# First attention of a six-stage block: softplus, triangular sums and exp, or sigmoids, a reversed scan and transposed blocks

## The reference, cut to what matters

```python
def stick_breaking_attention(q, k, v):
    """A[t,s] = beta_ts * prod_{s<j<t}(1 - beta_tj), s < t."""
    for i in range(seq // Q_BLOCK):
        q0 = i * Q_BLOCK
        kv_len = q0 + Q_BLOCK
        z = jnp.einsum('bqhd,bkhd->bhqk', q[:, q0:kv_len], k[:, :kv_len]).astype(jnp.float32) * scale
        causal = k_pos < q_pos
        log_beta = jax.nn.log_sigmoid(z)
        log_1m = jnp.where(causal, log_beta - z, 0.0)
        later = lax.cumsum(log_1m, axis=3, reverse=True) - log_1m
        w = jnp.where(causal, jnp.exp(log_beta + later), 0.0)
        outs.append(jnp.einsum('bhqk,bkhd->bqhd', w.astype(v.dtype), v[:, :kv_len]))
```

## Time and profile before

| | |
|---|---|
| median of 3 runs | 1973.13 us (1972.97 to 1973.66) |
| the profiled execution | 1974.07 us, its span 1972.3 us |
| granted TensorE clock, mean | 0.997 |
| busy: TensorE, weight loads, VectorE, ScalarE, GpSimd | 1940.5, 1582.1, 1470.6, 953.6, 454.8 us |
| the first attention's loop over pairs | about 734 to 846 us of the span |

### The profile page before, as it was taken

The page is one execution under the profiler, slowest core; times in us unless marked ns, Lnnn a source line. Parts: engine busy times, 40 slices in busy tenths (PEclk is TensorE's granted clock), DMA queues, the critical chain, the costliest instruction groups (busy, mean ns, idle before and its releaser), DMA issues.

```text
span 1972.3 us, 27125 instructions
## 1 busy us (share of the span) xinstructions
PE 1940.5 (98%) x10176; PEld 1582.1 (80%) x10176; DVE 1470.6 (75%) x2123; ACT 953.6 (48%) x1541; POOL 454.8 (23%) x471
## 2 busy tenths in 40 slices
PE   9999999999999999999999999999999999999997
PEld 6777878898897776787889889788888888886666
DVE  8995477877785449757786778778778778437985
ACT  5574343333344348733333335565555555236774
POOL 4131100570171000010066036124333331000002
PEclk9999999999999999999999999999999999999998
DMA  8465322243233220022324224322222223322112
GB/s 291 112 140 161 106 77 97 64 145 92 75 108 117 87 95 11 1 88 86 99 75 145 86 70 115 91 71 59 86 85 77 81 65 107 98 79 72 36 38 75
DMA packets 84546, 180.57 MB, mean 92 GB/s; under 512 B 18240, under 2 KB 33984, under 8 KB 84416
## 3 DMA queue, kind: packets, MB, share of 16 engines
q1 hardware_dynamic: 80848, 172.08, 29.1%
q0 software_dynamic: 3424, 6.23, 1.2%
q10 hardware_dynamic: 144, 0.52, 0.1%
HBM read 171.53 MB, written 7.27 MB: 91 GB/s over the span
## 4 chain that ended last, share of the span: by engine, by line
PE 68%; DVE 18%; ACT 6%; issue 6%; DMA 1%; SPq 0%; DVEq 0%; ACTq 0%
PE psum L522 12%; PE psum L525 12%; PE psum L523 12%; DVE wl L418 3%; ACT wh L406 3%; PE psum L462 3%; PE psum L459 3%; PE psum L460 3%; PE psum L563 2%; PE psum L566 2%; PE psum L564 2%; PE psum L544 2%; PE psum L1090 1%; PE psum L1092 1%; PE psum L1091 1%
## 5 line engine op out<-in xcount | busy, mean ns | idle before, releaser
L418 DVE TENSOR_TENSOR wl<-raw,wh 128x1024 fp32r<-128x1024 f32 (+3 forms) x359 | 430.8, 1203 | 255.1 <-ACT wh L406 254.2
L522 PE MATMUL psum<-xh,wh 128*128 128x512 f32 x1376 | 543.2, 395 | 1.8 <-DVE xl L641 1.8
L525 PE MATMUL psum<-xh,wl 128*128 128x512 f32 x1376 | 537.0, 390 | 2.5 <-DVE wl L418 2.5
L523 PE MATMUL psum<-xl,wh 128*128 128x512 f32 x1376 | 535.7, 389 | 0.0
L406 ACT ACTIVATE wh<-raw 128x1024 fp32r<-128x1024 f32 (+3 forms) x359 | 345.0, 964 | 291.1 <-PE psum L525 98.9
L522 PEld LDWEIGHTS psum<-xh,wh 128*128 128x128 f32 x1376 | 258.4, 188 | 61.2 <-ACT wh L406 2.6
L525 PEld LDWEIGHTS psum<-xh,wl 128*128 128x128 f32 x1376 | 258.3, 188 | 60.2 <-DVE wl L418 6.3
L523 PEld LDWEIGHTS psum<-xl,wh 128*128 128x128 f32 x1376 | 258.4, 188 | 55.2 <-issue 2.4
L431 POOL TENSOR_TENSOR raw<-raw 128x256 f32<-128x256 f32 x78 | 74.0, 949 | 441.1 <-DMA raw<-d_w 441.1
L462 PE MATMUL psum<-fh,wl 128*128 128x256 f32 x546 | 154.9, 284 | 1.8 <-DVE wl L418 1.6
L459 PE MATMUL psum<-fh,wh 128*128 128x256 f32 x546 | 154.7, 283 | 1.2 <-DVE fl L965 1.0
(11 more groups left out here) (548 smaller groups left out, 3710.3 us busy)
## 6 DMA issues: line engine op xcount, KB each, us to landing
raw<-d_w SPq DMA_DIRECT2D x224, 512.0 KB, 3.6
raw<-d_w SPq DMA_DIRECT2D x126, 256.0 KB, 2.7
Mt<-d_kd SPq DMA_DIRECT2D x64, 64.0 KB, 2.5
raw<-d_w SPq DMA_DIRECT2D x8, 320.0 KB, 2.9
bc<-d_bc SPq DMA_DIRECT2D x8, 256.0 KB, 4.5
d_ud<-ust SPq DMA_DIRECT2D x8, 256.0 KB, 2.6
U<-d_ud POOLq DMA_DIRECT2D x64, 32.0 KB, 2.4
d_yd<-HY SPq DMA_DIRECT2D x64, 32.0 KB, 2.1
```

Of the source, the lines that this page charges most:

```text
L418: dve.e.tensor_tensor(K.wl[n % NH][:, 0:w], K.raw[n % RAW][:, o:o + w], K.wh[n % NH][:, 0:w].bitcast(F32), ALU.subtract).then_inc(K.S["lo" ...
L522: pe.e.matmul(b[:, :], WH[:, o:o + P], XH, start=(k == k0), stop=False)
L523: pe.e.matmul(b[:, :], WH[:, o:o + P], XL, start=False, stop=False)
L525: mm = pe.e.matmul(b[:, :], WL[:, o:o + P], XH, start=False, stop=(k == k1 - 1))
```

## The change

Query and key change places: a block n = 4p + i now is pair p and query block i, with the query on the partition and 128(i+1) keys on the columns, for both heads. So there are 32 blocks. For each: scores and mask (`scores_pe`), ScalarE's two sigmoids (`sigmoid_act`: beta to SBUF, 1 - beta in place in PSUM), a scan of products from the last key back on VectorE (`remain_dve`), GpSimd's multiply of beta by what is left (`weigh_pool`), transposes of the 128x128 blocks of both heads on TensorE into two fixed banks (`turn1_pe`), and a copy of them to `ww` (`turned_act`). `mix_pe` works per pair as before. The sums, their constants `tri`, the softplus and the high and low parts are gone. There are three beta buffers, two for what is left, two pairs of score banks and one pair of turn banks.

```diff
-def sums_pe(K, pe, p, part): ...
-def softplus_act(K, act, i): ...
-def weigh_act(K, act, i): ...
-def softplus_abs_dve(K, dve, p): ...
-def softplus_dve(K, dve, i): ...
+TURN_BANK, SPREAD_BANK = 4, 6
+def score_bank(n):
+    return 2 - n % 2 * 2
+def keys(n):
+    return P * (n % 4 + 1)
+def scores_pe(K, pe, n):
+    p, i = n // 4, n % 4
+    pe.wait_ge("kq", 8 + p + 1)
     for e in range(2):
+        take(pe, score_bank(n) + e, ("rem", n + 1))
+    for e in range(2):
+        r = slice(64 * e, 64 * e + 64)
+        pe.e.matmul(scores(K, n)[:, e, :], K.qT[r, p, i * P:(i + 1) * P], K.kT[r, p, 0:keys(n)], start=True, stop=False,
+                    skip_group_check=True)
+    for e in range(2):
+        mm = pe.e.matmul(scores(K, n)[:, e, i * P:(i + 1) * P], K.mkb[:, :], K.idb[:, :], start=False, stop=True,
                          skip_group_check=True)
     mm.then_inc(K.S["sc"], 1)
+def sigmoid_act(K, act, n):
+    z = scores(K, n)
+    act.wait_ge("sc", n + 1)
+    act.wait_ge("trn", n - 2)
+    act.other("sigmoid")
+    act.e.activation(beta(K, n), z, ACT.Sigmoid).then_inc(K.S["act"], act.up())
+    act.e.activation(z, z, ACT.Sigmoid, scale=-1.0).then_inc(K.S["sgm"], 1)
+def remain_dve(K, dve, n):
+    z, out = scores(K, n), K.left[n % 2]
+    dve.wait_ge("sgm", n + 1)
+    dve.wait_ge("wgt", n - 1)
+    for e in range(2):
+        mm = dve.e.tensor_tensor_scan(out[:, e, 0:keys(n)][:, ::-1], z[:, e, :][:, ::-1],
+                                      K.zero[:, 0:1].broadcast_to([P, keys(n)]), 1.0, ALU.mult, ALU.add)
+    mm.then_inc(K.S["rem"], 1)
+def weigh_pool(K, pool, n):
+    k = keys(n)
+    w = beta(K, n)[:, :, 0:k - 1]
+    pool.wait_ge("rem", n + 1)
+    pool.e.tensor_tensor(w, w, K.left[n % 2][:, :, 1:k], ALU.mult).then_inc(K.S["wgt"], 1)
+def turn1_pe(K, pe, n):
     for e in range(2):
+        take(pe, TURN_BANK + e, ("wg", n + 1))
+    pe.wait_ge("wgt", n + 1)
+    for e in range(2):
+        for j in range(n % 4 + 1):
+            c = slice(j * P, (j + 1) * P)
+            mm = pe.e.transpose(K.bank[TURN_BANK + e][:, c], beta(K, n)[:, e, c], K.con("ident"))
+    mm.then_inc(K.S["trn"], 1)
+def turned_act(K, act, n):
+    p, i = n // 4, n % 4
+    act.wait_ge("trn", n + 1)
+    act.wait_ge("mix", p - 1)
+    act.e.activation(K.ww[:, p % 2, :, i:4 * i + 1:3, :],
+                     K.psum[:, TURN_BANK:TURN_BANK + 2, 0:keys(n)].rearrange("p e (j c) -> p e j c", c=P),
+                     ACT.Copy).then_inc(K.S["wg"], 1)
...
-LATE_HEADS = {2: ((0, 0), (1, 1)), 3: ((2, 5), (3, 6))}
+LATE_HEADS = {7: 0, 9: 1, 11: 2, 13: 3}
 def att1_pe(K, pe):
...
+    for t in range(2, 32):
+        scores_pe(K, pe, t)
+        if t == 2:
             head_sums_pe(K, pe, 3, 7)
+        if t in LATE_HEADS:
+            head_spread_pe(K, pe, 3, LATE_HEADS[t], SPREAD_BANK)
+        if t >= 3:
+            turn1_pe(K, pe, t - 3)
+        if t % 4 == 0 and t >= 8:
+            mix_pe(K, pe, t // 4 - 2)
+    turn1_pe(K, pe, 29)
     x = x_of(K, pe, 5)
     last = product_steps(K, pe, "b_w_o", (0, 1), (2, 3), x, (("h", 17), ("h", 18)))
+    next(last)
+    turn1_pe(K, pe, 30)
+    mix_pe(K, pe, 6)
+    next(last)
+    next(last)
+    turn1_pe(K, pe, 31)
+    next(last)
+    next(last)
     mix_pe(K, pe, 7)
 def att1_act(K, act):
...
+    for t in range(2, 35):
+        if t < 32:
+            sigmoid_act(K, act, t)
+        if t == 4:
             head_rsqrt_act(K, act, 3)
+        if t >= 3:
+            turned_act(K, act, t - 3)
+        if t % 4 == 1 and t >= 9:
+            mixed_act(K, act, t // 4 - 2)
```

More of the change, by code:

```diff
@@ L345 @@
     + ["gcp", "conv", "fa", "gv", "fh", "fl"]
-    + ["hcp", "hsq", "hn", "hny", "hbc", "kq", "mk", "sc", "sp2", "spa", "spl", "sums", "wg", "mix", "vt"]
+    + ["hcp", "hsq", "hn", "hny", "hbc", "kq", "mk", "sc", "sgm", "rem", "wgt", "trn", "wg", "mix", "vt"]
     + ["mraw", "dtk", "mxs", "mset", "mseta", "msetp", "mci", "mcv", "mth", "mfin", "mz", "mzt", "mcbp", "mcb", "mtp", "mxt"]
@@ L1024, in ffn_pool, with scores, beta @@
     add_squares(K, pool, 2 + 2 * layer)
-SLOT = [(0, 1), (2, 3), (5, 6)]
-PART_AT = (1024, 2048, 0)
 VALUE_BANKS = {"w_kv": (4, 0), "w_kv_2": (0, 4)}
[L1036 to L1071, removed]
+TURN_BANK, SPREAD_BANK = 4, 6
[3 more added lines that the diff above has]
+    return P * (n % 4 + 1)
+def scores(K, n):
+    b = score_bank(n)
+    return K.psum[:, b:b + 2, 0:keys(n)]
+def beta(K, n):
+    return K.beta[n % 3].rearrange("p (e c) -> p e c", e=2)[:, :, 0:keys(n)]
 def values_pe(K, pe, name, x, base, between=()):
@@ L1191, in head_end_dve @@
     dve.wait_ge("hsq", n + 1)
-    dve.wait_ge("mk", 5)
+    dve.wait_ge("mk", 4)
     dve.e.scalar_tensor_tensor(out=dst, in0=dst, scalar=K.par("k_norm" if n < 8 else "q_norm"),
                                in1=K.bank[bank][:, :], op0=ALU.mult, op1=ALU.mult).then_inc(K.S["kq"], 1)
-def scores_pe(K, pe, p, part):
-    heads = [slice(0, 64), slice(64, 128)]
+def scores_pe(K, pe, n):
+    p, i = n // 4, n % 4
     pe.wait_ge("kq", 8 + p + 1)
[L1203 to L1230, removed]
-    for e in range(2):
-        mm = pe.e.matmul(part_psum(K, i + 1)[:, e, 0:P], K.idb[:, :], K.mkb[:, :], start=False, stop=False,
@@ L1279, in mix_pe @@
 def mix_pe(K, pe, p):
     take(pe, 7, ("xl", 8 * 5 + p + 1))
[L1281 removed]
+    pe.wait_ge("wg", 4 * p + 4)
     pe.wait_ge("vt", 8)
[L1283 to L1284 removed]
+    for j in range(4):
         for e in range(2):
[L1286 removed]
+            w = K.ww[:, p % 2, e, 4 * j:3 * j + 4, :].rearrange("p i c -> p (i c)")
             v = K.Vt["w_kv"][:, j, (2 * p + e) * 64:(2 * p + e + 1) * 64]
[L1288 removed]
+            mm = pe.e.matmul(K.bank[7][64 * e:64 * e + 64, j * P:T], v, w, start=(j == 0), stop=(j == 3),
@@ L1309, in weigh_act @@
-def weigh_act(K, act, i):
-    act.wait_ge("sums", i + 1)
-    act.wait_ge("mix", i // 3)
-    act.wait_ge("hbc", 16)
-    act.e.activation(part_of(K.ww, i), part_psum(K, i), ACT.Exp).then_inc(K.S["wg"], 1)
 def mixed_act(K, act, p):
@@ L1512, in att1_pool @@
 def att1_pool(K, pool):
+    for n in range(32):
+        weigh_pool(K, pool, n)
     add_squares(K, pool, 3)
```

132 lines of the change are left out of this document (28 added, 104 removed).

## The result

The changed kernel takes **2010.59 us** (median of 4 runs, 2008.83 to 2013.58) against 1973.24 for the kernel before on the same chip: ratio 1.0191, interval 1.0173 to 1.0208, +37.4 us. Forecast were 1986 us, +12.8, with a range up to 1993. The direction was right, the forecast size a third of what came.

What follows compares the result with a forecast made beforehand. Three nearly full engines made hand-over order decide; after the change, ScalarE and TensorE taking turns would bound it. Head +9.0, middle +6.6, tail -3.0 made 12.6, with the table change 12.8: 1986 us, range 1980 to 1993.

Steps and rivals of the forecast that it cites:

- The mechanism: Attention loop: two waits and in-order queues make ScalarE and TensorE alternate, never side by side; 12.66 us a pair against 10.91.
- rival (b): Attention loop: a counted wait is off the path; without the mix, period 10.9, total 1979 us; chances 0.05 and 0.07.
- Rival (a): Attention: engines overlap as busy times allow, ScalarE the bound at 7.7 us a pair, total 1954 us; chance 0.05.
- the signs that I named: Attention: period 12.4 to 13.4 us, ScalarE's waits ended by transposes, TensorE's by the copy, clock 1.00, scans 1.2 us.
- ScalarE's 70%: Attention: a sign of being right was ScalarE busy about 70%.
- The table change behind the stage: Ahead of the second feed-forward's norm: ScalarE's table change adds at most 0.3 us.
- rival (c): Attention: TensorE's clock falls all through, doubling its loop terms, some 42 us more, 2028 us; chance 0.04.
- Late q norms: First two periods of the middle: the four late norms of q add 0.6 us in all.
- Variance ends as late as the table change, which it so covers: Head norm: VectorE's variance behind scan 3 is covered by ScalarE's 1.28 us change to the logarithm's table.
- The table back lies beside it, 0.3 over: Head: ScalarE's table change back runs beside transposes of 0.92 us, adding only 0.3 us.
- Period 12.66: Attention loop: one pair takes 12.66 us from mix to mix, against 10.91 before.
- Tail -3.0: From mix 5 to the first output pair: 29.8 us instead of 32.8, so 3.0 us gained.

Runs made afterwards that it cites:

- e2: The changed kernel with a fourth beta buffer, one for each block size, so the sigmoid waits for transposes four blocks back: 1981.2 us, ratio 1.0039.
- e4: The changed kernel with the fourth beta buffer and the mix ahead of the transposes of its turn: 1976.1 us, ratio 1.0009.
- e9: e4 with the mix ahead of the scores, the head norm and late q norms moved, and product steps around block 29: 1970.9 us, ratio 0.9986.
- e10: The changed kernel with unread filler matmuls in TensorE's waits in loop, head and tail: 1995.5 us, ratio 1.0111.
- e1: The changed kernel with unread filler matmuls in TensorE's waits in the loop only: 1997.4 us, ratio 1.012.
- e11: e10 without the four late q norms, so its result is wrong and only its time counts: 1990.9 us.
- e12: e10 with the variance of the last head norm ahead of scan 3 on VectorE: 1994.6 us.

## Why the prediction was wrong

**Right.** The mechanism: three beta buffers and one pair of turn banks make ScalarE and TensorE take turns. Sign, order of the chain, ScalarE's waits ended by the transposes and TensorE's by the copy, GpSimd and the scan off the path, all as written; e2 shows the buffers to be the cause, and e4 beside e2 (10.07 against 10.66 us) that the mix stood in the loop, against rival (b). Rival (a), engines that overlap, is out for this kernel. e9 comes near to it, but with TensorE as the bound at 9.93 us a pair and not ScalarE at 7.7. Of the signs that I named, the order of waits held, and the period, the clock and ScalarE's 70% (53% here, 57% in e10 over the same 125 us) did not. The table change behind the stage was put at 0.3 at most; the first output pair is 39.2 us late (885.51 against 846.27) and the table load 39.6, so 0.4.

**The step that failed is the one on the clock, rival (c).** I wrote that the clock is 1.00 "even in the first stretch with 7.0 of 10 us busy" and took that for safety. A busy share from another stage says nothing of this one: e9 has 1.00 from 760 to 770 us with 6.70 of 10 us busy, the changed kernel 0.71 and 0.75 with 6.99. I also priced the rival as all or nothing (+42, 2028 us) with 0.04, and left the middle of it, a clock that goes up and down from one stretch of a pair to the next, without a price. That middle came: 14.6 of the 36.4 us, 10.2 of them in the first six mixes (24.4 us together instead of 14.2). The Trainium skill (TensorE: Matmul & The Clock Gate, A second HAM failure mode: psum-queue depth-cycling) describes short idle times between groups of matmuls with which the clock goes back and forth; e1 (0.82 to 0.95 when they are filled) and e2 (mixes of 4.07 and 2.37 us in one kernel) agree with it. I had cited only the part with one idle spell.

**At full clock the sum was short by 9.2 us** (21.8 in e10 against 12.6):
- Late q norms, "0.6 for the four": 4.3, of which 1.3 in the head (e11). +3.7.
- "Variance ends as late as the table change, which it so covers": the load waits for it. +1.3 (e12).
- "The table back lies beside it, 0.3 over": it stands behind a wait of 1.01, so about +1.0 (read from the rows, not tried alone).
- Period 12.66: 12.96, five times, +1.5.
- Scores of block 0 wait 0.62 us for the last head norms of the group before, whose banks they now take: +0.6, read from this row of the changed kernel:

```profile
737.87 0.49 PE L1188 MATMUL psum<-kT,qT 64*128 64x128 f32 x4 [0.62 <-DVE qT L1173]
```
- Tail -3.0: -1.9. Of the 1.1, by the times of e10, 0.3 came before mix 6 (15.00 us from mix 5 against 14.66), 0.2 between mix 6 and 7 (8.88 against 8.67), 0.1 to the output pair, and 0.4 is the table change, for which my sum had up to 0.3 beside the -3.0. Together 3.7 + 1.3 + 1.0 + 1.5 + 0.6 + 1.1 = 9.2.

With these terms right and the clock still at 1.00 I would have said 1995, outside my own range. What stays open: why the clock falls in one pair and not in the next of the same program (e2), and the two terms of 1.0 and 0.6 above, which were read from rows and not tried alone.

## What to carry to other kernels

When a change makes TensorE wait often for another engine, even for short times (here 15 waits for the copy from 770 to 850 us, the longest 1.8 us), price its clock as a term of its own, between nothing and TensorE's work on the path once more, and not as a remote rival; the largest matmul group behind the waits pays. Take turns out of a loop by counting buffers against the distance that the queues need: here one more, smaller buffer and a mix that lies in a wait gave back 34 of the 37 us (e4), part of it through the clock. Cheap small steps (a lone 32-row matmul, a table load) are priced from how they will stand in the new queue: alone or side by side, before or behind a wait.
